# A four-layer decoder trunk in one Trainium2 kernel: a new order for the first sublayer, and forget attention begun among its projections

## What is computed

```python
y = swiglu(rms_norm(h, g[0]), w_gate, w_up, w_down);  h = h + 0.5 * rms_norm(y, g[1])
u = rms_norm(h, g[2]);  y = mixer(u, ...);            h = h + rms_norm(y, g[3])
# swiglu: (silu(x @ w_gate) * (x @ w_up)) @ w_down, hidden size 2816
```

```python
q, k, v, f_logit = split(h @ w_in)
log_f = log_sigmoid(f_logit + b_f);  cum = cumsum(log_f, axis=tokens)
logits = q @ k.T * 64**-0.5 + cum[query] - cum[key]     # causal mask
out = softmax(logits) @ v @ w_out
```

## Time and profile before

| | us |
|---|---|
| median of 3 runs | 1046.33 (1045.99 to 1047.19) |
| the profiled execution, as timed | 1046.0 |
| its span, first to last instruction | 1044.2 |
| PE busy in it | 1021.7 (98%) |
| DVE busy | 646.9 (62%) |
| ACT busy | 518.5 (50%) |
| POOL busy | 119.2 (11%) |

### The profile page before, as it was taken

How to read it: one execution, slowest core, us unless ns; L and a number is a source line. 1 busy time by engine, 2 the same in 40 slices (tenths; PEclk the granted TensorE clock), 3 DMA queues, 4 the chain that set the end, 5 groups by cost and what they waited for, 6 DMA issues and landing times.

```text
span 1044.2 us, 14407 instructions
## 1 busy us (share of the span) xinstructions
PE 1021.7 (98%) x5995; PEld 878.4 (84%) x5995; DVE 646.9 (62%) x777; ACT 518.5 (50%) x709; POOL 119.2 (11%) x225
## 2 busy tenths in 40 slices
PE   6999999999999999999999999999999999999997
PEld 6888888898856898888889888888988789888886
DVE  4755565756696755656576555566577775556554
ACT  4545445544564554454455444446545655444542
POOL 0000000212252200000030000002133420000000
PEclk8999999999999999999999999999999999999999
DMA  8676775568303265655556665555564135555552
...
DMA packets 137926, 187.99 MB, mean 180 GB/s; under 512 B 7345, under 2 KB 120326, under 8 KB 137862
## 3 DMA queue, kind: packets, MB, share of 16 engines
...
...
HBM read 184.42 MB, written 1.07 MB: 178 GB/s over the span
## 4 chain that ended last, share of the span: by engine, by line
PE 90%; DVE 4%; POOL 2%; issue 1%; ACT 1%; DMA 1%; DVEq 0%; POOLq 0%; SPq 0%; ACTq 0%
PE ps L1123 88%; PE ps L1462 1%; DVE normed L787 1%; ACT work L533 1%; DMA raw<-in_ffn_w_gate 1%; DVE wlo L752 1%; POOL ms L402 1%; POOL rstd L404 1%; PE ps L1292 1%; DVE res L776 1%; DVE probT_buf L905 1%; POOL ms_half L398 0%; DVE normed L883 0%; DVE normed L768 0%; DVE work L883 0%
## 5 line engine op out<-in xcount | busy, mean ns | idle before, releaser
L744 DVE TENSOR_TENSOR wlo<-raw,whi 128x2048 fp32r<-128x2048 f32 x151 | 347.0, 2298 | 142.5 <-ACT whi L509 142.3
L1123 PE MATMUL ps<-xhl,whi 128*128 128x512 f32 (+1 forms) x1600 | 387.4, 384 | 0.0
L1123 PEld LDWEIGHTS ps<-xhl,whi 128*128 128x128 f32 x1600 | 283.1, 189 | 50.8 <-issue 1.7
L509 ACT ACTIVATE whi<-raw 128x2048 fp32r<-128x2048 f32 x151 | 288.2, 1909 | 18.1 <-DMA raw<-in_nsa_w_in 5.2
L1123 PEld LDWEIGHTS ps<-xhl,wlo 128*128 128x128 f32 x1600 | 215.7, 190 | 16.1 <-DVE wlo L752 1.7
L1123 PE MATMUL ps<-xhl,wlo 128*128 128x256 f32 (+1 forms) x1600 | 221.0, 282 | 0.9 <-DVE wlo L752 0.9
L1123 PE MATMUL ps<-whi,xhl 128*128 128x256 f32 (+1 forms) x640 | 136.3, 321 | 3.0 <-DVE xhl L795 3.0
L1123 PE MATMUL ps<-whi,hhi 128*128 128x512 f32 x320 | 124.9, 390 | 0.0
L1123 PE MATMUL ps<-wlo,hhi 128*128 128x512 f32 x320 | 124.9, 390 | 0.0
L1123 PE MATMUL ps<-whi,hlo 128*128 128x512 f32 x320 | 124.5, 389 | 0.0
L1123 PEld LDWEIGHTS ps<-whi,xhl 128*128 128x128 f32 x640 | 104.1, 193 | 12.4 <-DVE wlo L752 3.3
...
## 6 DMA issues: line engine op xcount, KB each, us to landing
raw<-in_ffn_w_down SPq DMA_DIRECT2D x44, 1024.0 KB, 4.9
raw<-in_ffn_w_gate SPq DMA_DIRECT2D x41, 1024.0 KB, 5.3
raw<-in_ffn_w_up SPq DMA_DIRECT2D x41, 1024.0 KB, 5.4
raw<-in_fox_w_in SPq DMA_DIRECT2D x10, 1024.0 KB, 5.3
raw<-in_nsa_w_in SPq DMA_DIRECT2D x8, 1024.0 KB, 5.4
raw<-in_nsa_w_out SPq DMA_DIRECT2D x4, 1024.0 KB, 5.1
raw<-in_fox_w_out SPq DMA_DIRECT2D x4, 1024.0 KB, 5.0
...
```

The costliest lines, as they stand in the source:

```text
L509: nc.scalar.activation(whi[:, u % RING, :], raw_of(u), ACT.Copy).then_inc(w_hi, 1)
L744: nc.vector.tensor_tensor(wlo[:, u % RING, :], raw_of(u), whi[:, u % RING, :].bitcast(F32), ALU.subtract).then_inc(w_lo, 1)
L1123: return nc.tensor.matmul(out_, l, r, start=start, stop=stop)
```

## The change

At the start: the norm weights of the first sublayer are loaded as one row of 4 KB on ACT's queue, and PE multiplies them with a row of ones into two PSUM banks, from which `norm_input` reads them. Units 0 and 1 are loaded in halves, both ahead of the second part of x; units 2 and 3 go ahead of the small tables. The first products (`first_tokens`) are ordered by what is ready first, DVE's and ACT's lists likewise, and the second tile's transposes stand behind unit 1's first tile. There are two and then three dummy products instead of eight.

In FoX: queries and keys alternate (q, k, q, k, ...), each in one tensor, and scores contract over 64 rows, the two heads of a pair on different halves. cum (with the sign turned) is written to DRAM by POOL and loaded back repeated on all partitions into `bias` (2 MB). DVE adds the mask to it (`masked`, four instructions of 128 x 1024; `near` holds the blocks of the first 128 tokens), and the logits' instruction adds this in place of the mask. The term cum[query] is left out, since the softmax doesn't change by it. Three score groups stand ahead of projections 9, 10 and 11, and DVE, ACT and POOL handle these three stages among the projections.

```diff
-                    load_cols(u0, w_gate[i, m], 0)
+                    for u, w in ((u0, w_gate[i, m]), (u0 + 1, w_up[i, m])):
+                        if s == 0:
+                            for b in range(2):
+                                sp.dma_start(raw[:, u, 1024 * b:1024 * b + 1024].rearrange("p (k n) -> p k n", k=4),
+                                             w[512 * b:512 * b + 512, 0:UC].rearrange("(k p) n -> p k n", p=P)).then_inc(raw_in[u] if b else first_in[u], 16)
+                        else:
+                            load_cols(u, w, 0)
                     if s == 0:
                         load_x(1)
-                    load_cols(u0 + 1, w_up[i, m], 0)
-                    if s == 0:
-                        load_small()
                     for c in range(1, NCH):
                         load_cols(gate_unit(u0, c), w_gate[i, m], c * UC)
                         load_cols(gate_unit(u0, c) + 1, w_up[i, m], c * UC)
+                        if s == 0 and c == 1:
+                            load_small()
...
                     w, wo = (nsa_in[0], nsa_out[0]) if kind == "nsa" else (fox_in[0], fox_out[0])
-                    cols = [1792, 2304, 1024, 1280, 0, 256, 1536, 2048, 512, 768] if kind == "nsa" else [UC * k for k in (8, 9, 10, 11, 0, 1, 2, 3, 4, 5, 6, 7)]
+                    cols = [1792, 2304, 1024, 1280, 0, 256, 1536, 2048, 512, 768] if kind == "nsa" else [UC * k for k in (8, 9, 10, 11, 0, 4, 1, 5, 2, 6, 3, 7)]
...
             nc.gpsimd.memset(half[:, :], -0.5).then_inc(half_set, 1)
-            load_gain(0, 0)
             pool.wait_ge(half_set, 1)
             for t in range(TT):
                 rstd_of(0, 0, t)
...
                 if KINDS[s] == "fox":
-                    pool.wait_ge(wide_ready, 1)
-
-                    for h in range(H):
-                        o_ = slice(64 * (1 - h % 2), 64 * (1 - h % 2) + 64)
-                        last = nc.gpsimd.tensor_scalar(qF[h % 2][o_, h // 2, :], cum_wide[o_, :], cst[o_, C_A1 + h:C_A1 + h + 1],
-                                                       cst[o_, C_A2 + h:C_A2 + h + 1], ALU.mult, ALU.add)
-                    last.then_inc(decay_ready, 1)
+                    pool.wait_ge(cum_ready, 1)
+                    pool.dma_start(scratch[:, 0:S], cum[0:H, :]).then_inc(cum_out, 16)
+                    pool.wait_ge(cum_out, 16)
+                    pool.dma_start(bias[:, :, :], bass.AP(scratch.tensor, 0, [[0, P], [SCORES, H], [1, S]])).then_inc(decay_in, 16)
                     for n in range(H, H + H // 2):
                         scale_probs(n)
                 between_sublayers(s)
...
             def hi_part(u, b):
                 cols = slice(1024 * b, 1024 * b + 1024)
-                if b == 0:
+                if u < 2:
+                    act.wait_ge(raw_in[u] if b else first_in[u], 16)
+                elif b == 0:
                     raw_here(u)
                 nc.scalar.activation(whi[:, u % RING, cols], raw_of(u)[:, cols], ACT.Copy).then_inc(w_hi if b else part_hi, 1)
...
                 n0, p0, N = STAGE0[kind], PAIR0[kind], STAGES[kind]
                 per = 2 if kind == "nsa" else 1
...
-                for i in range(N + LAG + 2):
+                for i in range(EARLY_STAGES[kind], N + LAG + 2):
                     if i >= LAG + 2 and (i - LAG - 1) % per == 0:
                         heads_hi((i - LAG - 1) // per - 1)
                     if i < N:
-                        exps(n0 + i)
...
+            i, n = NORM[0]
+            act.dma_start(gain_row[:, :], bass.AP(norm_g.tensor, (i * 6 + n) * D, [[0, 1], [1, D]])).then_inc(gain_row_in, 16)
             act.dma_start(ident, consts[:, C_ID:C_ID + P]).then_inc(ident_in, 16)
 
             square_x(0)
@@ -648,8 +657,9 @@
             for b in range(2):
                 hi_part(0, b)
             split_x(0, 0)
+            for b in range(2):
+                hi_part(1, b)
             square_x(1)
-            hi(1)
             split_x(0, 1)
...
                             act.wait_ge(proj_ready, PROJ0[kind] + k - 1)
+                            if kind == "fox" and k == 8:
+                                act.wait_ge(cum_ready, 1)
                             scale = DH ** -0.5 if is_query(kind, k) else 1.0
-                            nc.scalar.activation(cross_sb(k), cross_of(bank), ACT.Copy, scale=scale).then_inc(cross_ready, 1)
...
                         evacuate(k - 1)
                         if k > 1:
                             hi(u0 + k + 2)
+                        if kind == "fox" and k >= 9:
+                            exps(kind, H + k - 9)
...
                 if t == 0:
-                    dve.wait_ge(gpre_in, 16 * (s + 1))
+                    if s == 0:
+                        dve.wait_ge(gain_mm, 1)
+                    else:
+                        dve.wait_ge(gpre_in, 16 * s)
                 dve.wait_ge(res_in[t] if s == 0 else res_ready, 16 if s == 0 else TT * (s - 1) + t + 1)
                 dve.wait_ge(rstd_ready, i + 1)
-                for cols in (slice(0, 512), slice(512, 1024)):
-                    nc.vector.scalar_tensor_tensor(normed[:, t, cols], res[:, t, cols], rstd[:, i:i + 1], g_pre[:, cols],
+                for b in range(2):
+                    cols = slice(512 * b, 512 * b + 512)
+                    g_ = g_pre[:, cols] if s else ps[:, OB + b, :]
+                    nc.vector.scalar_tensor_tensor(normed[:, t, cols], res[:, t, cols], rstd[:, i:i + 1], g_,
                                                    ALU.mult, ALU.mult).then_inc(normed_ready, 1)
...
+            def logits(kind, n):
+                b = n % PB
+                dve.wait_ge(scores_mm, n + 1)
+                if kind == "fox" and n in (H, H + 4):
+                    dve.wait_ge(decay_ready, 2 if n == H else 4)
+                if n >= PB:
+                    dve.wait_ge(probT_mm, n - PB + 1)
+                for a in range(2):
+                    for t, (c0, c1) in enumerate(((0, P), (P, SCORES))):
+                        j0 = P if t == 0 else 0
+                        if kind == "nsa":
+                            add = bias_at(2 * (n // 2) + a, j0, S - j0, 1)
+                        else:
+                            h = 2 * (n - H) + a
+                            add = bias[:, h, :] if t else near[h // KT][:, h % KT, :]
+                        last = nc.vector.tensor_tensor_reduce(
+                            out=prob[b][:, a, c0:c1], in0=ps[:, 2 * (n % 2) + a, c0:c1], in1=add, scale=-1.0, scalar=3e38,
+                            op0=ALU.add, op1=ALU.min, accum_out=nmax[:, b, a, t:t + 1])
+                last.then_inc(logits_ready, 1)
...
-                for i in range(N + LAG + 2):
+                for i in range(EARLY_STAGES[kind], N + LAG + 2):
                     if i < N:
-                        logits(n0 + i)
+                        logits(kind, n0 + i)
...
+            nc.vector.memset(ones_row[:, :], 1.0).then_inc(ones_set, 1)
             norm_input(0, 0)
+            lo_part(0, 0)
+            split_x(0, 0)
+            lo_part(0, 1)
             for b in range(2):
-                lo_part(0, b)
-            split_x(0, 0)
+                lo_part(1, b)
             norm_input(0, 1)
-            lo(1)
             split_x(0, 1)
...
                         else:
-                            halves, c = (qF, 2 * (k - 4)) if k < 8 else (kFs, 2 * (k - 8))
-                            for r in range(2):
-                                o_ = slice(64 * r, 64 * r + 64)
-                                last = nc.vector.scalar_tensor_tensor(halves[r][o_, c:c + 2, :], m_[o_], scale, c_[o_], ALU.mult, ALU.add)
-                            last.then_inc(proj_ready, 1)
+                            c = 2 * ((k - 4) // 2)
+                            dst = (kF if k % 2 else qT)[:, c:c + 2, :]
+                            nc.vector.scalar_tensor_tensor(dst, m_, scale, c_, ALU.mult, ALU.add).then_inc(proj_ready, 1)
+
+                    def masked(dst, src):
+
+                        m_ = cst[:, C_MASK + P:C_MASK + S]
+                        m_h = bass.AP(m_.tensor, m_.offset, [list(m_.ap[0]), [0, KT], [1, P]])
+                        nc.vector.tensor_tensor(dst, src, m_h, ALU.add).then_inc(decay_ready, 1)
                     lo(u0 + 3)
                     for k in range(1, nproj - 1 if kind == "nsa" else nproj):
                         join(k - 1)
+                        if kind == "fox" and k == 4:
+                            dve.wait_ge(f_ln, 1)
+                            nc.vector.scalar_tensor_tensor(fT[:, 1, :], fT[:, 0, :], 0.0, fT[:, 3, :], ALU.min, ALU.subtract).then_inc(f_step, 1)
+                            dve.wait_ge(f_step, 3)
+                            nc.vector.memset(zeros, 0.0).then_inc(f_step, 1)
+                            dve.wait_ge(f_step, 4)
+                            nc.vector.tensor_tensor_scan(cum[:, :], zeros, fT[:, 1, :], 0.0, ALU.add, ALU.subtract).then_inc(cum_ready, 1)
```

(74 more changed lines are left out.)

98 lines of the change are left out of this document (41 added, 57 removed).

## The result

The changed kernel takes 1037.5 us, the median of six runs (1037.07 to 1038.16), against 1046.16 for six runs of the kernel before (1045.88 to 1047.25): a ratio of 0.9915 with an interval of 0.9905 to 0.9925, or 8.7 us less. Forecast were 9.6 us less. The profiled execution took 1037.07 us, with a span of 1035.3.

The account below looks back on a forecast made before the run. PE was taken as the bound, busy 1021.7 of 1044.2 us. 1046.3 less 4.3 at the start and 5.3 in FoX gave 1036.7; the forecast's own range was 1034 to 1038, with rivals 1 and 2 1034 to 1041.5.

Parts of the forecast that it names:

- either bound: Start: PE's work on the gain row begins between 3.2 and 4.8 us; 3.6 was taken.
- DVE's list: Start: DVE's instructions set the stretch; PE waits for unit 1's last low half until 14.6 us.
- rival 1: Start: PE's granted clock isn't full well before 12 us; the start brings only 2.1, time 1038.9 us; chance 0.13.
- the measured 20.8: FoX before the change: us from the projections' end (801.31) to 822.12, set against 15.5 in the new order.
- narrow contraction: FoX: scores over 64 rows instead of 128 save 0.55 us in each of 8 stages, 4.4, less 0.3.
- The bias as a broadcast: FoX: the PE product that widens cum is removed, saving 0.6 us.
- The interleaving: FoX: three score groups go among the projections at 2.6 us; gain is what is left of waits of 0.72 and 1.00.
- the floor: FoX stages: DVE's work allows no stage under 2.46 us; 2.45 was taken.
- the new wait: FoX: PE waits 1.1 us for DVE before the second transposes.
- the cover: FoX: the 2 MB bias lands at 772 to 776, at worst 780, early enough to cost nothing.
- Rival 3: FoX: the broadcast is late and DVE stands before its low halves; slower than before, about 1049 us; chance 0.04.
- Rivals 2 and 4: 2: FoX gains only 1.4, 1040.6 us, chance 0.13. 4: start's and FoX's gains are given back, about 1046, chance 0.03.

Follow-up runs that it names:

- the changed kernel's second profile: The changed kernel run once more with nothing changed, as the measure for two kernels beside it: 1037.43 us, ratio 0.9919.
- the wide kernel: The changed kernel, but each FoX score product contracts over all 128 rows, summing both heads of a pair: 1039.1 us, ratio 0.9941 to the kernel before.

## Why the prediction was right, point by point

**The sum.** 9.6 us were forecast and 8.7 measured; 1037.5 lies within the forecast's own range. By the profiles the start brought 3.8 where 4.3 was forecast, FoX 5.1 where 5.3 was, and all else nothing, as forecast.

**Start, gain row.** PE began on it at 2.86, earlier than either bound (3.2 and 4.8), and the normalisation began at 6.89 (7.1 forecast). The lower bound was taken from x's landing less the time of its bytes; the row was there before that.

**Start, what sets the stretch: the mechanism was wrong.** The forecast has DVE's list set it, with PE waiting for unit 1's low half. The low halves did end when told (14.43; 14.6 forecast), but PE's own list set the stretch. It had no pause from its first product at 10.30 to 16.14, and unit 1's first tile ended there (15.5 forecast). The forecast's own numbers don't give 15.5 either: 12.8 and 24 products of 0.12 are 15.7. The first 24 ended at 13.26, and not near 12.8. DVE's wait of 0.79 for POOL's scale was missing too, but it ended just before PE was free. From the end of the products to the second tile it took 2.11 (2.0 forecast), so the second tile began at 18.25 (17.5) and unit 1 ended at 24.07 (23.6). The bare transposes cost 0.92 of PE's standing, the tables nothing: both as forecast. That the number came near with the wrong engine as the bound is luck: DVE's list and PE's differ here by a few tenths.

**Start, the clock (rival 1).** Full from 12.5 at the latest in every profile of the new start, where the kernel before was at half rate from 13.66 to 17.80. The rival did not come about, though the forecast's limit of 12 was passed by 0.3 in the changed kernel's second profile. What I hadn't seen is the spread of up to 1 us between executions of one kernel.

**FoX, the sum was right and its terms were not.** The sum was not added up from the terms: it lays the new order out step by step and takes it from the measured 20.8. Counted from the place where the projections ended before (66.31 us behind the normalisation), the steps came out: projections' end 2.4 (2.0 forecast), second transposes 6.0 (5.8), transposes of stage 5 15.65 (15.5). The first is late because three narrow groups between projections cost 3 x 1.05 = 3.2 and not 2.6.

The step that failed is the division of the gain. The *narrow contraction* was put at 4.4 less 0.3 and measured 2.5. The price of a wide group was taken from one place, behind the products with the values (1.41), and multiplied by eight. Among the projections narrow saves 0.26 a group, not 0.55; behind the last one 0.45; and the kernel before has groups of 1.31 at its head. In addition the faster kernel pays 0.67 us more of the wait before the second transposes (0.96 against 0.29). *The bias as a broadcast* was put at 0.6, the widening product alone, and measured 1.6: the shorter join, 0.7 us ahead of the first transposes (7.39 to 6.65), was overlooked. *The interleaving* was put at what was left, 0.6, and measured 1.1 with wide scores and 1.4 with narrow ones, before what it spares of the clock. Had one of the three parts been forecast alone, it would have come out wrong, as the expectation for the wide kernel did.

**FoX, the floor.** Stages of 2.46 where 2.45 was forecast; the new wait 0.96 where 1.1 was; first transposes right behind the fourth group. The forecast has DVE as the floor. DVE is full in the third stage, but PE's own products fill all three as well, so these rows don't say which of the two sets them. The Trainium skill's factor of up to 2 (TensorEngine Tiling (Array Packing), Theoretical Speedup) would be 0.70 us a group, an estimate; every narrow group here takes 0.86, so the row decides. In the stages even 0.70 would have brought little, since DVE is busy there for up to 2.46 of 2.46.

**FoX, the cover.** The load took 12.6 us where the row for it said 10.0, and a unit beside it up to 9.8 us, for which ACT waited 3.68 and PE nothing. The forecast's times are those of the kernel before; counted from the FoX normalisation (735.00 there, 731.19 here) the load landed at 39.3, within the 37 to 41 of the forecast. Its terms give less, 34.8 to 38.8 (cum at 23.8, the write 1 to 5, the load 10.0); cum was ready at 24.0 and the load issued at 26.7, and the longer load filled the difference. Rival 3's mechanism is real, and its threshold came out near, 53.3 against 54.0, but for another reason: it is the join that PE wants first, and not the low half.

**Rivals 2 and 4** are out: groups take 0.86 and stages 2.46, and the halves of the change add up.
